# A decoder trunk on one core: a stage for turning the cumulated gates, and a retimed table of small stages

## The chip, the cores and the metric

The kernel runs on one core of one Trainium2 chip. The metric is the device time of one execution in microseconds (us); the median of three runs of the kernel before is 866.67 us (866.63 to 866.77). An execution of this kernel repeats closely, so that a change of 0.2% (1.7 us) can be told from none.

## The reference, cut to what matters

Two layers, 256 tokens, width 1024, all in float32. Each layer is one wide projection, four token mixers, gated sums, an output projection and a SwiGLU block:

```python
proj = einsum('bsd,dn->bsn', rms_norm(x), w_in)        # n = 7428 columns
u, dq, dk, dv, sq, sk, sv, fq, fk, fv, f_logit, g_logit = split(proj)
o_pool = pool_mixer(u); o_diff = diff_attention(dq, dk, dv)
o_sb = stick_breaking(sq, sk, sv)
# forgetting attention: the cumulated log gates are added to the scores
cum = cumsum(log_sigmoid(f_logit + b_forget))
logits = fq_n @ fk_n.T * scale + cum[q] - cum[k]
o_fox = softmax(causal(logits)) @ fv
merged = sum_n sigmoid(g_n + b_gate) * (o_n @ w_branch_n)
x = x + merged @ w_out
h = rms_norm(x); gate, up = split(h @ w_up); x = x + (silu(gate) * up) @ w_down
```

## The kernel before, in words

**Weights and slots.** The weights of one layer are cut into 144 units. A unit is two blocks of 128 rows by 512 columns (260 columns for one item), 512 KB. SyncE loads it into `raw`; ScalarE rounds it into `w_hi` (`split_hi`, L718), VectorE subtracts to get the remainder `w_lo` (`split_lo`, L977), and TensorE multiplies: high by high, high by low, low by high (L1636, L1637, L1640), for both halves of the tokens. That makes 12 matmuls of 512 columns for a unit. The products go into `bulk`, four PSUM banks. The number of a unit in its layer is also the number of its slot. A ring of five buffers (`RING`) holds the split weights: ScalarE splits unit g+4 only when TensorE is done with unit g-1, and VectorE splits unit g+4 at the end of its own slot g.

**Small stages between the units.** Everything that is not a bulk product is a stage: transposes, scores, softmax, evacuations. The tables `MIXING_PE`, `MIXING_ACT` and `MIXING_DVE` say in which slot each engine does its part of which stage. On TensorE the stages of a slot come before the unit of that slot. On ScalarE and VectorE they come before the split of unit g+4. Each engine does its list strictly in order, so an entry that has to wait holds back all behind it, the splits too. The four PSUM banks of the small stages are called A, B, T and O; `take` makes TensorE wait until the last reader of a bank is done with it.

**The stages that the change touches.** `tr_ss` and `ss_evac` turn and evacuate the queries and keys of stick-breaking attention (the four instructions at L1172 and L1174 on VectorE). At slot 8 of layer 0 VectorE also makes the masks (five casts, L1347 and L1349). `tr_fox` turns the forgetting queries (`fq`) or keys (`fk`) into bank A (L1414), and next to them the cumulated gates, `forget_rows`, into bank B (L1415); ScalarE and VectorE evacuate both (`fox_evac`). `scores`, `maxima`, `softmax`, `tr_probs`, `probs_evac`, `pv` and `pv_evac` are the steps of attention, for four `diff` heads and two pairs of `fox` heads. `sigmoid` opens the gates on ScalarE. `tr_diff` and `diff_evac` turn the normalized output of the diff heads. GpSimd turns heads with rotary embedding (L656 to L663) and adds the four gated branches, six additions for each half j of the columns (L690). The additions for the last branch signal `merged_ready`, once for each half t of the tokens. `tr_merged` j waits for `merged_ready` (j, 0), turns that half into one bank, then waits for `merged_ready` (j, 1) and turns the other (L1567). Units 74 to 77 are the first that multiply what `tr_merged` 1 turned.

Of the kernel before, what the change touches and what calls it, by code (L numbers as in the profile page):

```python
# [122 lines left out]
def timetable(*entries):  # L123
# [9 lines left out]
    (32, "scores", "diff", 1), (32, "pv", "diff", 0), (34, "cum"), (34, "pool_a"), (34, "scores", "diff", 2),
    (35, "tr_probs", "diff", 1), (36, "scores", "diff", 3), (36, "pool_b"), (36, "pv", "diff", 1),
    (37, "tr_probs", "diff", 2), (38, "tr_fox", "fq"), (38, "pv", "diff", 2), (39, "tr_fox", "fk"),
    (40, "tr_probs", "diff", 3), (42, "scores", "fox", 0), (42, "pv", "diff", 3), (45, "tr_probs", "fox", 0),
    (45, "scores", "fox", 1), (46, "pv", "fox", 0), (50, "tr_probs", "fox", 1), (52, "tr_diff", 0), (52, "tr_diff", 1),
# [1634 lines left out]
```

## Time and profile before

| | us |
|---|---|
| median of 3 runs | 866.67 |
| the profiled execution, its own time | 866.5 |
| the profiled execution, span from first to last instruction | 864.7 |
| TensorE busy | 860.1 (99%) |
| VectorE busy | 599.4 (69%) |
| ScalarE busy | 441.4 (51%) |
| GpSimd busy | 110.1 (13%) |

The span begins at the first instruction, so all starts below count from there. A busy TensorE row is read with care: matmuls overlap, and the modelled duration of one (0.39 us at 512 columns) is longer than the step from one start to the next (0.23 us). What a matmul costs is that step, not its duration. A short wait can hide in this overlap without showing as idle time.

### The profile page before, as it was taken

Reading aid. Unit: us, or ns where it says so; the run is one execution under the profiler, and the core shown is the slowest. Engines: PE = TensorE matmul, PEld = TensorE weight load, DVE = VectorE, ACT = ScalarE, POOL = GpSimd, SP = SyncE. Lnnn points to the kernel's source line nnn. Section 1 sums busy time; section 2 is a strip of 40 time slices with the busy share of each in tenths; the row PEclk is TensorE's granted clock in tenths of the full one; section 3 lists DMA queues with packets and bytes.
Section 4 is the critical chain, followed back from the end, with each engine's and each line's share of the span. In section 5 each row is a group of like instructions: output and inputs, shape, how many; then the busy total and the mean of one; then the engine's idle time right before and its main releaser. Section 6 shows DMA issues by size and latency. Waiting matters only on the chain.

```text
span 864.7 us, 11127 instructions
## 1 busy us (share of the span) xinstructions
PE 860.1 (99%) x4247; PEld 712.1 (82%) x4247; DVE 599.4 (69%) x847; ACT 441.4 (51%) x639; POOL 110.1 (13%) x89
## 2 busy tenths in 40 slices
PE   9999999999999999999999999999999999999998
PEld 7888888888888888888888888888888888888886
DVE  5996887768777556654479868777597765565542
ACT  6556564754454444443375574556543644444431
POOL 0740100004501000000005401000064000000000
PEclk9999999999999999999999999999999999999999
DMA  9656565575657666555665455655666476665541
GB/s 331 201 185 179 173 189 171 161 236 183 207 171 237 192 178 190 192 175 193 171 184 166 130 183 168 194 176 175 210 195 193 127 238 177 190 185 181 194 146 50
DMA packets 87366, 159.48 MB, mean 184 GB/s; under 512 B 7432, under 2 KB 13712, under 8 KB 87312
## 3 DMA queue, kind: packets, MB, share of 16 engines
q1 hardware_dynamic: 87152, 158.69, 59.1%
q8 instruction: 34, 0.56, 0.2%
q14 instruction: 20, 0.16, 0.1%
q10 hardware_dynamic: 160, 0.07, 0.0%
HBM read 157.69 MB, written 1.05 MB: 184 GB/s over the span
## 4 chain that ended last, share of the span: by engine, by line
PE 99%; DMA 0%; DVE 0%; issue 0%
PE bulk L1636 30%; PE bulk L1640 30%; PE bulk L1637 30%; PE bankAB L1386 2%; PE bulk L1667 1%; PE bankAB L1577 1%; PE bankT L1530 0%; PE bankAB L1519 0%; DMA con<-consts_dram 0%; PE bankAB L1477 0%; PE bankAB L1395 0%; PE bankO L1490 0%; PE bankO L1548 0%; PE bankO L1577 0%; PE bankT L1577 0%; PE bankO L1395 0%
## 5 line engine op out<-in xcount | busy, mean ns | idle before, releaser
L977 DVE TENSOR_TENSOR w_lo<-raw,w_hi 128x1024 fp32r<-128x1024 f32 (+1 forms) x288 | 361.6, 1268 | 162.4 <-ACT w_hi L718 159.8
L718 ACT ACTIVATE w_hi<-raw 128x1024 fp32r<-128x1024 f32 (+1 forms) x288 | 299.0, 1048 | 237.5 <-PE bulk L1640 233.7
L1636 PE MATMUL bulk<-w_hi,hT_hi 128*128 128x512 f32 (+1 forms) x884 | 346.5, 392 | 0.0
L1637 PE MATMUL bulk<-w_lo,hT_hi 128*128 128x512 f32 (+1 forms) x884 | 340.8, 386 | 0.0
L1640 PE MATMUL bulk<-w_hi,hT_lo 128*128 128x512 f32 (+1 forms) x884 | 338.1, 386 | 0.0
L1640 PEld LDWEIGHTS bulk<-w_hi,hT_lo 128*128 128x128 f32 x884 | 165.7, 188 | 33.8
L1636 PEld LDWEIGHTS bulk<-w_hi,hT_hi 128*128 128x128 f32 x884 | 166.1, 188 | 33.3 <-issue 1.6
L1637 PEld LDWEIGHTS bulk<-w_lo,hT_hi 128*128 128x128 f32 x884 | 166.2, 188 | 31.4
L1636 PE MATMUL bulk<-w_hi,aT_hi 128*128 128x512 f32 x176 | 68.8, 391 | 0.0
L1640 PE MATMUL bulk<-w_hi,aT_lo 128*128 128x512 f32 x176 | 68.5, 389 | 0.0
L1637 PE MATMUL bulk<-w_lo,aT_hi 128*128 128x512 f32 x176 | 68.5, 389 | 0.0
L690 POOL TENSOR_TENSOR wide<-wide 128x512 f32<-128x512 f32 x24 | 46.1, 1943 | 125.2 <-DVE wide L1262 124.8
L656 POOL TENSOR_TENSOR wide<-wide,ropeA 128x512 f32<-128x512 f32 x8 | 12.0, 1494 | 210.9 <-DVE wide L1069 210.9
L1640 PEld LDWEIGHTS bulk<-w_hi,aT_lo 128*128 128x128 f32 x176 | 33.0, 188 | 7.0
L1637 PEld LDWEIGHTS bulk<-w_lo,aT_hi 128*128 128x128 f32 x176 | 33.0, 188 | 6.8
L1636 PEld LDWEIGHTS bulk<-w_hi,aT_hi 128*128 128x128 f32 x176 | 33.0, 188 | 6.7
L1636 PE MATMUL bulk<-w_hi,oT_hi 128*128 128x512 f32 x80 | 31.3, 391 | 0.0
L1640 PE MATMUL bulk<-w_hi,oT_lo 128*128 128x512 f32 x80 | 31.1, 389 | 0.0
L1637 PE MATMUL bulk<-w_lo,oT_hi 128*128 128x512 f32 x80 | 31.1, 389 | 0.0
L914 ACT ACTIVATE wide<-bulk,y_ffn 128x512 f32<-128x512 f32 (+1 forms) x24 | 14.4, 651 | 18.2 <-PE bulk L1640 16.0
L1252 DVE SCALAR_TENSOR_TENSOR wide<-bulk,y_attn,bias 128x512 f32<-128x512 f32 x32 | 22.5, 744 | 1.4 <-PE bulk L1640 1.4
L1276 DVE SCALAR_TENSOR_TENSOR wide<-bulk,y_ffn,wide 128x512 f32<-128x512 f32 (+1 forms) x24 | 15.9, 702 | 10.2 <-ACT wide L914 10.2
(259 smaller groups left out, 711.7 us busy)
## 6 DMA issues: line engine op xcount, KB each, us to landing
raw<-in_w_in_dram SPq DMA_DIRECT2D x112, 512.0 KB, 4.4
raw<-in_w_ffn_up_dram SPq DMA_DIRECT2D x80, 512.0 KB, 4.4
raw<-in_w_ffn_down_dram SPq DMA_DIRECT2D x44, 512.0 KB, 3.3
raw<-in_w_branch_dram SPq DMA_DIRECT2D x20, 512.0 KB, 4.1
raw<-in_w_out_dram SPq DMA_DIRECT2D x16, 512.0 KB, 3.3
bias<-in_b_gate_dram SPq DMA_DIRECT2D x16, 256.0 KB, 4.9
raw<-in_w_ffn_up_dram SPq DMA_DIRECT2D x16, 256.0 KB, 3.4
raw<-in_w_in_dram SPq DMA_DIRECT2D x8, 256.0 KB, 2.6
```

The lines of the kernel that those rows point to most:

```text
L656: pool.tensor_tensor(ta, x, ropeA[:, i, t:t + 1, :].broadcast_to([P, 8, HD]), ALU.mult)
L690: ins = pool.tensor_tensor(m, m, wide[:, t, n * D + j * NC:n * D + (j + 1) * NC], ALU.add)
L718: act.activation(w_hi[:, g % RING, :, 0:width], raw[:, g % RAW, :, 0:width], ACT.Copy).then_inc(hi_ready, 1)
L914: act.activation(ff_tmp(t, p, width), item_bank(layer, ITEM_AT[item], t)[:, 0:width], ACT.Sigmoid, scale=y_ffn[:, t:t + 1]).then_inc(ff_si ...
L977: vec.tensor_tensor(w_lo[:, g % RING, :, 0:width], raw[:, g % RAW, :, 0:width], w_hi[:, g % RING, :, 0:width].bitcast(F32), ALU.subtract). ...
L1252: vec.scalar_tensor_tensor(out=wide[:, t, g * NC:(g + 1) * NC], in0=item_bank(layer, ITEM_AT[("gate", g)], t), scalar=y_attn[:, t:t + 1], ...
L1276: vec.scalar_tensor_tensor(out=s, in0=item_bank(layer, ITEM_AT[item], t)[:, 0:width], scalar=y_ffn[:, t:t + 1], in1=s, op0=ALU.mult, op1=A ...
L1386: ins = pe.matmul(dst, a[a_part], b[b_part], start=start and a_part + b_part == 0, stop=stop and a_part == 1, skip_group_check=True)
L1577: ins = pe.transpose(bank[name][:, k * P:(k + 1) * P], ff_act(t, p, blocks * P)[:, k * P:(k + 1) * P], identity)
L1636: pe.matmul(dst, hi, whi, start=(k == ks[0]), stop=False)
L1637: pe.matmul(dst, hi, wlo, start=False, stop=False)
L1640: ins = pe.matmul(dst, lo, whi, start=False, stop=(k == ks[-1]))
```

## The change

1. The gates leave `tr_fox`. It turns queries into bank A and keys into bank B, four transposes each, and no longer waits for the gates. A new stage `tr_forget` turns the gates into bank T, four transposes, with its own evacuation `forget_evac` (two ScalarE copies) and its own signal `forgetsT_ready`, for which the fox scores wait. The numbers of transposes and copies are the same as before.
2. Stages move in the three tables. On TensorE the stages of slots 34 to 54 stood in 13 slots and stand in 9. `tr_qk` dq and `sb_scores` 0 change places in slot 14. `tr_merged` 1 moves from slot 73 to 72. On VectorE `ss_evac` moves from 9 to 7, and in the region from 34 to 56 entries change places. On ScalarE the first `sigmoid` comes ahead of the exponentials of the second pair of fox heads.

The diff, cut to its core; of the tables, the entries named above and a few around them:

```diff
 MIXING_PE = [
-    (9, "tr_ss"), (14, "sb_scores", 0), (14, "tr_qk", "dq"), ...
+    (9, "tr_ss"), (14, "tr_qk", "dq"), (14, "sb_scores", 0), ...
...
-    (54, "pv", "fox", 1), (68, "tr_merged", 0), (73, "tr_merged", 1)]
+    (55, "pv", "fox", 1), (68, "tr_merged", 0), (72, "tr_merged", 1)]
...
 MIXING_ACT = [
-    ... (42, "softmax", "fox", 0), (45, "probs_evac", "fox", 0), (46, "softmax", "fox", 1),
-    (46, "sigmoid", 0, 0), (48, "pv_evac", "fox", 0), (48, "sigmoid", 0, 1), ...
+    ... (42, "softmax", "fox", 0), (44, "probs_evac", "fox", 0),
+    (46, "sigmoid", 0, 0), (47, "softmax", "fox", 1), (48, "pv_evac", "fox", 0), (48, "sigmoid", 0, 1), ...
...
 MIXING_DVE = [
-    (5, "qk_norm", "dq"), (7, "lambda_sums"), (9, "ss_evac"), (10, "lambdas"), ...
+    (5, "qk_norm", "dq"), (7, "lambda_sums"), (7, "ss_evac"), (10, "lambdas"), ...
...
-    (40, "gate", 2), (41, "maxima", "fox", 0),
-    (42, "pv_evac", "diff", 3), (42, "softmax", "fox", 0), (44, "gate", 3), ...
+    (40, "gate", 2), (41, "maxima", "fox", 0),
+    (41, "softmax", "fox", 0), (42, "pv_evac", "diff", 3), (43, "gate", 3), ...
...
+            def forget_evac(layer):
+                act.wait_ge(stage_done, nth(stage_done, layer, ("tr_forget",)))
+                act.activation(forgetsT["fq"], bank["T"][:, 0:SEQ], ACT.Copy)
+                act.activation(forgetsT["fk"], bank["T"][:, SEQ:2 * SEQ], ACT.Copy).then_inc(forgetsT_ready, 1)
...
             def tr_fox(layer, which):
-                pe.wait_ge(forget_out, nth(forget_out, layer, "aug"))
                 pe.wait_ge(rotated, nth(rotated, layer, (which, 1)))
-                take("AB", qkT_ready, layer, which)
+                name = {"fq": "A", "fk": "B"}[which]
+                take(name, qkT_ready, layer, which)
                 for t in range(TT):
                     for pair in range(2):
                         at = pair * SEQ + t * P
-                        pe.transpose(bank["A"][:, at:at + P], foxes[which][:, t, pair * P:(pair + 1) * P], identity)
-                    ins = pe.transpose(bank["B"][:, t * P:(t + 1) * P], forget_window[which, t], identity)
+                        ins = pe.transpose(bank[name][:, at:at + P], foxes[which][:, t, pair * P:(pair + 1) * P], identity)
                 ins.then_inc(stage_done, 1)
...
+            def tr_forget(layer):
+                pe.wait_ge(forget_out, nth(forget_out, layer, "aug"))
+                take("T", forgetsT_ready, layer, "both")
+                for i, which in enumerate(("fq", "fk")):
+                    for t in range(TT):
+                        at = i * SEQ + t * P
+                        ins = pe.transpose(bank["T"][:, at:at + P], forget_window[which, t], identity)
+                ins.then_inc(stage_done, 1)
...
             def scores(layer, kind, h):
...
+                if kind == "fox":
+                    pe.wait_ge(forgetsT_ready, nth(forgetsT_ready, layer, "both"))
```

TensorE around `tr_merged` 1 (transposes out of `wide` into T and O, each waiting for `merged_ready`), before:

```order
L1636 MATMUL bulk<-w_hi,hT_hi 128x512
L1637 MATMUL bulk<-w_lo,hT_hi 128x512
L1640 MATMUL bulk<-w_hi,hT_lo 128x512
L1567 MATMUL bankT<-con,wide 128x128 [waits lhs_lo,merged_ready]
L1567 MATMUL bankT<-con,wide 128x128 x3
L1567 MATMUL bankO<-con,wide 128x128 [waits lhs_lo,merged_ready]
L1567 MATMUL bankO<-con,wide 128x128 x3
L1636 MATMUL bulk<-w_hi,hT_hi 128x512 [waits lo_ready]
```

The same place now:

```order
L1653 MATMUL bulk<-w_hi,hT_hi 128x512
L1654 MATMUL bulk<-w_lo,hT_hi 128x512
L1657 MATMUL bulk<-w_hi,hT_lo 128x512
L1584 MATMUL bankT<-con,wide 128x128 [waits lhs_lo,merged_ready]
L1584 MATMUL bankT<-con,wide 128x128 x3
L1584 MATMUL bankO<-con,wide 128x128 [waits lhs_lo,merged_ready]
L1584 MATMUL bankO<-con,wide 128x128 x3
L1653 MATMUL bulk<-w_hi,hT_hi 128x512 [waits gated,lo_ready]
```

The eight transposes now stand ahead of unit 72, whose first matmul is the one that waits for `gated`; before, unit 72 stood ahead of them. Between the two `tr_merged` stages there were five units, now there are four.

VectorE from slot 7 to slot 10 of layer 0, before (L977 are the splits of units 11, 12 and 13, `keys_lo` is `ss_evac`, `small` belongs to `lambda_sums`, the casts make the masks):

```order
L1098 TENSOR_REDUCE small<-wide 128x2 [waits vec_step]
L977 TENSOR_TENSOR w_lo<-raw,w_hi 128x1024 [waits hi_ready]
L1347 CAST masks<-con 128x128 [waits consts_loaded]
L1347 CAST masks<-con 128x128 x2
L1349 CAST sums<-con 128x128 x2
L977 TENSOR_TENSOR w_lo<-raw,w_hi 128x1024 [waits hi_ready]
L1172 SCALAR_TENSOR_TENSOR keys_lo<-bankT,keys_hi 128x2x128 [waits sT_hi]
L1174 TENSOR_TENSOR keys_lo<-bankT,keys_hi 128x2x128
L1172 SCALAR_TENSOR_TENSOR keys_lo<-bankO,keys_hi 128x2x128 [waits sT_hi]
L1174 TENSOR_TENSOR keys_lo<-bankO,keys_hi 128x2x128
L977 TENSOR_TENSOR w_lo<-raw,w_hi 128x1024 [waits hi_ready]
```

The same place now:

```order
L1104 TENSOR_REDUCE small<-wide 128x2 [waits vec_step]
L1178 SCALAR_TENSOR_TENSOR keys_lo<-bankT,keys_hi 128x2x128 [waits sT_hi]
L1180 TENSOR_TENSOR keys_lo<-bankT,keys_hi 128x2x128
L1178 SCALAR_TENSOR_TENSOR keys_lo<-bankO,keys_hi 128x2x128 [waits sT_hi]
L1180 TENSOR_TENSOR keys_lo<-bankO,keys_hi 128x2x128
L983 TENSOR_TENSOR w_lo<-raw,w_hi 128x1024 [waits hi_ready]
L1353 CAST masks<-con 128x128 [waits consts_loaded]
L1353 CAST masks<-con 128x128 x2
L1355 CAST sums<-con 128x128 x2
L983 TENSOR_TENSOR w_lo<-raw,w_hi 128x1024 [waits hi_ready] x2
```

The four instructions of `ss_evac` now stand ahead of the splits of units 11 and 12.

ScalarE around the second pair of fox heads (`sb,den<-bankAB` are its exponentials, `wide<-wide` the sigmoids), before:

```order
L870 ACTIVATE sb,den<-bankAB,nmx 128x256 [waits probs_ready,maxed]
L872 ACTIVATE sb,den<-bankAB,nmx 128x128
L870 ACTIVATE sb,den<-bankAB,nmx 128x256
L872 ACTIVATE sb,den<-bankAB,nmx 128x128
L896 ACT_TABLE_LOAD
L896 ACTIVATE wide<-wide 128x1024 [waits gate_ready]
```

Now:

```order
L902 ACT_TABLE_LOAD
L902 ACTIVATE wide<-wide 128x1024 [waits gate_ready]
L719 ACTIVATE w_hi<-raw 128x1024 [waits unit_done,raw_loaded2]
L876 ACT_TABLE_LOAD [waits probs_ready]
L876 ACTIVATE sb,den<-bankAB,nmx 128x256 [waits maxed]
L878 ACTIVATE sb,den<-bankAB,nmx 128x128
L876 ACTIVATE sb,den<-bankAB,nmx 128x256
L878 ACTIVATE sb,den<-bankAB,nmx 128x128
L719 ACTIVATE w_hi<-raw 128x1024 [waits unit_done,raw_loaded3]
L723 ACTIVATE oT_hi<-bankO 128x256 [waits stage_done]
L902 ACT_TABLE_LOAD
```

A sigmoid now stands between two sets of exponentials, and two more table loads stand in each layer.

## Rows read from the trace of the kernel before

**Rows 1.** Page, parts 1 and 2: busy times; granted clock in tenths, 40 slices.

```profile
PE 860.1 (99%) x4247; PEld 712.1 (82%) x4247; DVE 599.4 (69%) x847; ACT 441.4 (51%) x639; POOL 110.1 (13%) x89
...
PEclk9999999999999999999999999999999999999999
```

**Rows 2.** Waits of TensorE: line, waited for, us in total, times, longest.

```profile
PE bulk L1674 <- DVE warm L1311: 1.0, 1, 1.0
```

**Rows 3.** Timeline of TensorE, slots 72, 73, and 73 of layer 1: start us, us, engine, line, operation.

```profile
230.27 0.39 PE L1636 MATMUL bulk<-w_hi,hT_hi 128*128 128x512 f32 x1
...
233.00 0.60 PE L1567 MATMUL bankT<-con,wide 128*128 128x128 f32 x4
233.43 0.60 PE L1567 MATMUL bankO<-con,wide 128*128 128x128 f32 x4
233.79 0.47 PE L1636 MATMUL bulk<-w_hi,hT_hi 128*128 128x512 f32 x1
...
660.00 0.60 PE L1567 MATMUL bankT<-con,wide 128*128 128x128 f32 x4
```

**Rows 4.** Timeline of GpSimd, the last addition of half 1, layers 0 and 1.

```profile
229.59 2.27 POOL L690 TENSOR_TENSOR wide<-wide 128x512 f32<-128x512 f32 x1
...
656.59 2.28 POOL L690 TENSOR_TENSOR wide<-wide 128x512 f32<-128x512 f32 x1
```

**Rows 5.** Timeline of VectorE, the split beside the addition of layer 0.

```profile
228.90 1.81 DVE L977 TENSOR_TENSOR w_lo<-raw,w_hi 128x1024 fp32r<-128x1024 f32 x1 [0.42 <-ACT w_hi L718]
```

**Rows 6.** Timeline of VectorE, slots 7 to 9 of layer 0.

```profile
36.97 2.00 DVE L977 TENSOR_TENSOR w_lo<-raw,w_hi 128x1024 fp32r<-128x1024 f32 x1
...
40.27 0.21 DVE L1347 CAST masks<-con 128x128 bf16<-128x128 f32 x1
40.41 1.31 DVE L1349 CAST sums<-con 128x128 fp32r<-128x128 f32 x1
...
41.77 1.21 DVE L977 TENSOR_TENSOR w_lo<-raw,w_hi 128x1024 fp32r<-128x1024 f32 x1
42.91 0.41 DVE L1172 SCALAR_TENSOR_TENSOR keys_lo<-bankT,keys_hi 128x256 fp32r<-128x256 f32 x1
...
44.24 1.21 DVE L977 TENSOR_TENSOR w_lo<-raw,w_hi 128x1024 fp32r<-128x1024 f32 x1
```

**Rows 7.** Timeline of GpSimd beside them (rotary embedding).

```profile
36.55 1.35 POOL L656 TENSOR_TENSOR wide<-wide,ropeA 128x512 f32<-128x512 f32 x1
...
40.34 1.29 POOL L663 TENSOR_TENSOR wide<-wide 128x512 f32<-128x512 f32 x1
```

**Rows 8.** Timeline of TensorE's weight loads and matmuls, start of unit 12.

```profile
43.04 0.19 PEld L1636 LDWEIGHTS bulk<-w_hi,hT_hi 128*128 128x128 f32 x1
...
43.16 0.40 PE L1636 MATMUL bulk<-w_hi,hT_hi 128*128 128x512 f32 x1
```

**Rows 9.** Timeline of TensorE, the first two matmuls after the transposes of slot 39.

```profile
130.97 0.47 PE L1636 MATMUL bulk<-w_hi,hT_hi 128*128 128x512 f32 x1
131.28 0.39 PE L1637 MATMUL bulk<-w_lo,hT_hi 128*128 128x512 f32 x1
```

**Rows 10.** Timeline of VectorE, the divisions (`softmax`) of fox pairs 0 and 1.

```profile
144.34 0.18 DVE L1197 RECIPROCAL inverse<-den 128x4 f32<-128x4 f32 x1 [0.32 <-ACT sb L872]
...
146.65 2.35 DVE L977 TENSOR_TENSOR w_lo<-raw,w_hi 128x1024 fp32r<-128x1024 f32 x2
...
159.87 0.17 DVE L1197 RECIPROCAL inverse<-den 128x4 f32<-128x4 f32 x1
...
161.00 0.42 DVE L984 TENSOR_TENSOR oT_lo<-bankO,oT_hi 128x256 fp32r<-128x256 f32 x1
```

**Rows 11.** Timeline of TensorE, `tr_probs` of fox pair 0 in slot 45.

```profile
150.00 0.49 PE L1530 MATMUL bankT<-con,sb 128*128 128x128 f32 x3
```

**Rows 12.** Timeline of ScalarE, end of the exponentials and the table load.

```profile
155.16 0.22 ACT L872 ACTIVATION_READ_ACCUMULATOR sb<-bankAB,nmx 128x1 f32 x1
155.39 1.28 ACT L896 ACT_TABLE_LOAD   x1
```

More of the change, by code:

```diff
@@ L130 @@
 MIXING_PE = [
-    (9, "tr_ss"), (14, "sb_scores", 0), (14, "tr_qk", "dq"), (18, "sb_sums", 0), (20, "sb_out", 0), (20, "sb_scores", 1),
+    (9, "tr_ss"), (14, "tr_qk", "dq"), (14, "sb_scores", 0), (18, "sb_sums", 0), (20, "sb_out", 0), (20, "sb_scores", 1),
     (23, "sb_sums", 1), (24, "tr_qk", "dk"), (25, "sb_out", 1), (25, "scores", "diff", 0), (29, "tr_probs", "diff", 0),
[L133 to L137, printed above, removed]
-    (54, "pv", "fox", 1), (68, "tr_merged", 0), (73, "tr_merged", 1)]
+    (32, "scores", "diff", 1), (32, "pv", "diff", 0), (35, "cum"), (35, "pool_a"), (35, "scores", "diff", 2),
+    (35, "tr_probs", "diff", 1), (37, "scores", "diff", 3), (37, "pool_b"), (37, "pv", "diff", 1),
+    (39, "tr_probs", "diff", 2), (39, "tr_fox", "fq"), (39, "tr_fox", "fk"), (39, "pv", "diff", 2), (39, "tr_forget"),
+    (42, "tr_probs", "diff", 3), (42, "scores", "fox", 0), (42, "pv", "diff", 3), (44, "tr_probs", "fox", 0),
+    (46, "pv", "fox", 0), (46, "scores", "fox", 1), (51, "tr_probs", "fox", 1), (53, "tr_diff", 0), (53, "tr_diff", 1),
+    (55, "pv", "fox", 1), (68, "tr_merged", 0), (72, "tr_merged", 1)]
 _PE = [(0, "tr_norm", "attn", 0, 1)] + MIXING_PE + [(F0, "tr_norm", "ffn", 0, 1)]
@@ L210 @@
-    (50, "probs_evac", "fox", 1), (52, "diff_evac", 0), (52, "diff_evac", 1), (52, "sigmoid", 2, 0),
-    (54, "pv_evac", "fox", 1), (54, "sigmoid", 2, 1), (60, "sigmoid", 3, 0), (61, "sigmoid", 3, 1), (69, "merged_evac", 0),
+    (36, "pool_evac_a"), (36, "probs_evac", "diff", 1), (36, "softmax", "diff", 2), (37, "pool_evac_b"),
+    (38, "softmax", "diff", 3), (38, "probs_evac", "diff", 2), (39, "fox_evac", "fq"), (39, "fox_evac", "fk"),
+    (39, "forget_evac"), (41, "probs_evac", "diff", 3), (42, "softmax", "fox", 0), (44, "probs_evac", "fox", 0),
@@ L486, in build @@
         qkT_ready = signal("qkT_ready", turned)
+        forgetsT_ready = signal("forgetsT_ready", ["both"])
         qkT_hi = signal("qkT_hi", turned)
@@ L1162, in fox_evac @@
                 high, low = (part[:, 0:2, :] for part in qT[which])
-                vec.tensor_tensor(low, bank["A"].rearrange("p (h q) -> p h q", h=2), high.bitcast(F32),
-                                  ALU.subtract).then_inc(qkT_ready, 1)
+                src = bank[{"fq": "A", "fk": "B"}[which]].rearrange("p (h q) -> p h q", h=2)
+                vec.tensor_tensor(low, src, high.bitcast(F32), ALU.subtract).then_inc(qkT_ready, 1)
             def ss_evac(layer):
@@ L1305, in _ @@
                           sb_mask=sb_mask, fox_norm=fox_norm,
-                          sb_weights=nothing, sb_evac=sb_evac, fox_evac=fox_evac, fkfv=nothing, dv=nothing,
+                          sb_weights=nothing, sb_evac=sb_evac, forget_evac=nothing, fox_evac=fox_evac, fkfv=nothing, dv=nothing,
                           softmax=softmax, probs_evac=nothing, pv_evac=pv_evac, diff_norm=diff_norm,
@@ L1578, in tr_act @@
                     ins.then_inc(stage_done, 1)
-            stages = dict(tr_norm=tr_norm, tr_qk=tr_qk, tr_fox=tr_fox, tr_ss=tr_ss, cum=cum, pool_a=pool_a, pool_b=pool_b,
+            stages = dict(tr_norm=tr_norm, tr_qk=tr_qk, tr_fox=tr_fox, tr_forget=tr_forget, tr_ss=tr_ss, cum=cum, pool_a=pool_a, pool_b=pool_b,
                           sb_scores=sb_scores, sb_sums=sb_sums, sb_out=sb_out, scores=scores, tr_probs=tr_probs, pv=pv,
```

38 lines of the change are left out of this document (18 added, 20 removed).

## Prediction

> **What bounds the kernel.** I read the busy times first. TensorE is at work for 860.1 of 864.7 us, VectorE for 69%, ScalarE for 51%, and the granted clock is at its full 2.4 GHz level in all forty slices [rows 1]. Then the waits: all that TensorE ever waited for in a way that shows is 1.0 us at the start, ahead of the warm-up [rows 2]. So nothing can be won by making another engine faster, and an edit acts in two ways only: it changes what TensorE has to do, or it makes TensorE wait where it did not. The profiled execution took 866.5 us; I sum against that and carry the sum to the median, 866.67.
>
> Then the timelines, for how close each hand-over is. The price of a bulk matmul is the step between starts. From 230.27 to 233.00 lie the twelve of unit 72: 2.73 us, 0.23 each [rows 3]. A slot without stages is 2.73 us long, and this is the unit in which I move things.
>
> **The edit itself: gates in bank T.** Per layer, twelve transposes stay twelve and four ScalarE copies stay four; matmuls and bytes are the same. What changes is what waits for what. The new wait of the fox scores for `forgetsT_ready` ends two slots before the scores: `tr_forget` stands in slot 39, the scores in slot 42, and between them lie three units, 8.2 us, for two copies. Behind `forget_evac` on ScalarE stands the split of unit 43, with four units' time to spare. I cost this edit at nothing. Its cover is those three units; without it the copies, under 1 us, would be paid.
>
> **Fewer visits.** TensorE leaves the bulk products for the stages of slots 34 to 54 thirteen times a layer, then nine times. Going back costs something: the first matmul after transposes takes 0.31 us to the next start (130.97 to 131.28) where 0.23 is usual [rows 9], so 0.08 us. Bounds for a visit saved: below, nothing (the last transpose before the unit may be started past more quickly and give it back); above, 0.2, if going in costs as much as coming out and a little more. I take 0.08, the row's own number: 4 visits x 2 layers x 0.08 = 0.64 us won, between 0 and 1.6. The swap in slot 14 leaves the number of visits alone: nothing.
>
> **`tr_merged` 1, one slot earlier.** It turns the two halves of the merged gates, four transposes each. Before, the first group starts at 233.00 and the second at 233.43 [rows 3], and the second needs GpSimd's last addition, which ends at 229.59 + 2.27 = 231.86 [rows 4]: 1.57 us to spare. In layer 1 it ends at 658.87, and the first group starts at 660.00 [rows 3, 4]: in either layer the addition ends 1.13 to 1.14 us ahead of the first group. Unit 72 was the cover. Now the first group starts at 230.27, in place of that unit. Its addition is done by 229.59, when the last one starts. The second group comes 0.43 later, at 230.70, and waits until 231.86. A weight load then follows 0.06 us behind a release and the first matmul 0.12 behind the load: unit 12 shows it, 42.98 to 43.04 to 43.16 [rows 6, 8]. So it starts at 232.04 and not at 230.70: 1.34 us lost, which no later place gives back, since TensorE has no idle time into which it could be pushed.
>
> Is the addition tied to TensorE, so that it doesn't come earlier too? GpSimd's additions wait for VectorE's products with the gates, and these wait for units 65 to 69; the tables leave that order alone. The split beside the last addition itself waits for ScalarE (0.42 us), which waits for TensorE [rows 5]. So the whole chain moves with TensorE. Per layer 1.34 us, with bounds 1.1 (the release is seen at once, and the weight load is hidden) and 1.4; two layers: 2.7 us.
>
> **`ss_evac` ahead of two splits.** VectorE's four instructions take 44.24 - 42.91 = 1.33 us [rows 6]. They now run at 36.97, before the splits of units 11 and 12. Their input is there (ScalarE has evacuated the same banks by then). In layer 0 the split of unit 12 ends at 41.77 + 1.21 = 42.98, the weight load starts at 43.04 and the matmul at 43.16, just 0.23 after its predecessor's start: not late, but with nothing to spare [rows 6, 8]. Above, the whole 1.33 is paid. Below, nothing: much of VectorE's time here is waiting. The split at 36.97 takes 2.00 us where 1.21 is usual, and ends 1.07 after GpSimd's instruction that began at 36.55 ended at 37.90. One cast takes 0.21, the next 1.31, up to 41.72, just behind the end of GpSimd's instruction at 40.34 + 1.29 = 41.63 [rows 6, 7]. So an instruction of VectorE that reads SBUF waits for the one of GpSimd that is running. `ss_evac` reads PSUM beside SBUF and took its plain time. While it runs, GpSimd gets ahead: behind 37.90 it has two instructions of half width and the one of 1.29, some 2.8 us, and the split of unit 11 holds it up for 1.1, so it is done at about 41.8 (an estimate from these rows). By then two of the five casts are through, three follow at 0.21, and the split of unit 12 begins at about 42.2 and ends at about 43.4. Loss: 0.4 us, the value I take, between 0 and 1.33. In layer 1 there are no casts in this place, and unit 12's split has several us to spare: nothing.
>
> [...]
>
> **Slots 34 to 56.** I followed each hand-over with the steps above. The closest new one is in slot 44. `tr_probs` of fox pair 0 moves from 150.00 [rows 11] to about 147.2, and needs bank O, so VectorE's copy of the last diff head's output. In the VectorE list that copy now stands behind the division of pair 0 and the split of unit 45, which were behind it. The exponentials end at 144.3; the division takes 1.13 if it runs as for pair 1 (159.87 to 161.00), 2.31 if as for pair 0 (144.34 to 146.65) [rows 10]; split and copy take 1.2 + 0.4. That gives 147.0 or 148.2. The division of pair 0 was slow because GpSimd's squares ran beside it, and these wait for that same copy, so they can't now. I take 147.0: nothing lost. The other end is 1.0 us a layer. The next closest is `pv` of diff head 2 in slot 39, in the same slot as its `tr_probs`; eight transposes of `tr_fox` (0.9 us) lie between and cover the evacuation.
>
> **Sum.** -0.64 + 2.68 + 0.4 = +2.4 us: 868.9 for a profiled execution, 869.1 as a median.
>
> **Rivals.**
> (a) *The addition is done in time: not slower.* Should GpSimd's last additions take 1.3 us like its instruction at 40.34 [rows 7], and not 2.27, the last two end 1.9 us sooner, at about 229.9, before 230.70. Then nothing is paid in slot 72, and -0.64 + 0.4 remains: 866.4, no change. It decides if the additions are done by 230.6. For it: VectorE's entries before shift, and its split beside the addition (1.81 us and not 1.21 [rows 5]) shows that the two hold each other up. Against it: the lists of both engines after slot 60 are untouched, and the two layers agree to 0.01 us. 10%.
> (b) *The copy in slot 44 is late too.* As above with the slow division, 0.5 to 1.0 a layer: 870 to 871.1. 10%.
> (c) *The table loads.* ScalarE now changes tables three times, not once, around the second fox pair. A load takes 1.28 us and begins as the exponentials end (155.38 to 155.39) [rows 12]. Two more are 2.6 us of ScalarE, which was idle longer than that between slots 42 and 50, and the fox probabilities of pair 1 then come about 1.7 us before slot 51 needs them: nothing. If loads cost twice that, TensorE waits 1 to 2 us a layer in slot 51: 871 to 873. 4%.
> The Trainium skill, "ScalarE: Activation LUTs", section "What ACT_TABLE_LOAD costs", puts a switch at 2.66 us, 1.28 for the load and as much again for a drain. The row shows the load and no drain before it, so I keep (c) small.
> (d) *Fewer visits count for more,* with (a)'s additions in time: faster by over 0.2%. 3%.
>
> **Chances and range.** The forecast's mechanism, `merged_ready` late in slot 72 in both layers, has 73%. Its own range goes from 2.2 - 1.6 + 0 = +0.6 to 2.8 + 1.33 = +4.1, and I believe its middle: 868 to 870.5. With (b) above and part of (a) below: 867.3 to 871. A difference of 0.2% (1.7 us, so above 868.4 or below 864.9) is what can be told from none. Slower: nearly all of the forecast (68 of 73), (b) and (c), 80%. No change: (a) and the forecast's low end, 17%. Faster: 3%.
>
> **What would show it.** In the profile after, the waits of TensorE list L1584 waiting for GpSimd's L690, once a layer. A modelled matmul end hides some of it, so the starts tell more: from the first group of `tr_merged` 1 to the second, about 1.8 us and not 0.43. In layer 0 the step into unit 12 is 0.6 us and not 0.23, in layer 1 it is 0.23. There is no step over 0.4 us at slots 39, 44 and 51. From slot 34 to slot 56 TensorE takes some 0.3 us less in each layer. The prediction is wrong if the second group follows the first without a gap, or if a gap stands anywhere else.

## The result, and the profile after

The changed kernel takes 868.52 us (median of 14 runs, 868.38 to 868.96), the kernel before 866.56 (14 runs, 866.25 to 866.78): 1.96 us or 0.23% more, a ratio of 1.0023 with a 95% interval of 1.0016 to 1.0030. It is slower, as forecast, by 1.96 us where 2.4 were forecast. The profiled execution took 868.38 us, with a span of 866.6, against 866.5 and 864.7.

The page of the changed kernel, beside [rows 1], shows TensorE at work for 99% of the span again; ScalarE has four instructions more, the table loads.

```profile
PE 859.9 (99%) x4247; PEld 712.7 (82%) x4247; DVE 594.5 (69%) x847; ACT 447.3 (52%) x643; POOL 111.7 (13%) x89
```

The list of TensorE's waits of the changed kernel (us in total, times, longest) has a new first line beside [rows 2]: the second group of `tr_merged` 1 waits for GpSimd's addition, once in each layer. The other two lines are of the start of the program. The kernel before has both as well, the second with 0.4 us (`consts_dram`), which the prediction left out when it put all of TensorE's visible waiting at 1.0.

```profile
PE bankO L1584 <- POOL wide L691: 2.1, 2, 1.0
PE bulk L1691 <- DVE warm L1317: 1.0, 1, 1.0
PE bankO L1697 <- DMA con<-consts_dram: 0.5, 1, 0.5
```

The timelines of GpSimd, TensorE and its weight loads in slot 72 of the changed kernel, and one row of layer 1, answer to [rows 3, 4]:

```profile
229.26 2.25 POOL L691 TENSOR_TENSOR wide<-wide 128x512 f32<-128x512 f32 x1
...
229.94 0.60 PE L1584 MATMUL bankT<-con,wide 128*128 128x128 f32 x4
231.57 0.66 PE L1584 MATMUL bankO<-con,wide 128*128 128x128 f32 x4 [1.03 <-POOL wide L691]
231.98 0.47 PE L1653 MATMUL bulk<-w_hi,hT_hi 128*128 128x512 f32 x1
...
231.57 0.42 PEld L1584 LDWEIGHTS bankO<-con,wide 128*128 128x128 f32 x4 [1.26 <-POOL wide L691]
...
659.56 0.66 PE L1584 MATMUL bankO<-con,wide 128*128 128x128 f32 x4 [1.02 <-POOL wide L691]
```

The addition ends at 229.26 + 2.25 = 231.51, and 0.06 later the second group starts, 1.63 us behind the first and not 0.43. The wait shows as 1.03 only, because the modelled end of the first group covers the rest: the steps are what to read. From unit 9 to unit 143 of either layer this is also the only place of the changed kernel where two starts of TensorE in a row lie over 0.35 us apart; in the kernel before there is none.

Where does the time go? Most of it can be told by the first matmul of a unit: a stretch between two such starts repeats within 0.04 us in kernels that don't differ there; the one exception behind the start-up is the 2.7 us from unit 12 to 13 of layer 0, which varies by 0.06. From the timelines of TensorE of both kernels, in us:

| units | before | after | difference | what differs there |
|---|---|---|---|---|
| start to 9, layer 0 | 34.90 | 34.65 | -0.25 | start-up, 34.65 to 35.17 over all kernels here |
| 9 to 16, layer 0 | 21.04 | 21.27 | +0.23 | `ss_evac`, slot 14 |
| 16 to 32 | 47.81 | 47.86 | +0.05 | entries of slots 16 to 21 |
| 32 to 56 | 82.11 | 81.74 | -0.37 | the visits, the gates |
| 56 to 68 | 33.43 | 33.43 | 0 | |
| 68 to 74 | 17.35 | 18.60 | +1.25 | `tr_merged` 1 |
| 0 to 143, layer 1 | | | +0.98 | the same, without `ss_evac` |

In layer 0 that is +1.16 from unit 9 on, in layer 1 +0.98; with the start-up's -0.25 it makes 1.89 of 1.88 us (868.38 - 866.5). The start-up differs by up to 0.5 us between the profiled executions, also among kernels that are the same up to there, so differences of 0.1 or 0.2 us are read from the stretches and not from the whole time.

### The profile page after: what moved, and what is told of

Same layout as the page of the kernel before. It is cut to its first block, busy times and chain, and to the rows that moved or that the text cites. A ratio compares the mean times of both kernels' runs of the same rounds, so it can differ in the third digit from the quotient of the medians.

```text
span 866.6 us, 11133 instructions
## 1 busy us (share of the span) xinstructions
PE 859.9 (99%) x4247; PEld 712.7 (82%) x4247; DVE 594.5 (69%) x847; ACT 447.3 (52%) x643; POOL 111.7 (13%) x89
## 4 chain that ended last, share of the span: by engine, by line
PE 96%; DVE 1%; POOL 1%; issue 1%; DMA 0%; POOLq 0%
PE bulk L1653 29%; PE bulk L1657 29%; PE bulk L1654 29%; PE bankAB L1392 2%; PE bulk L1684 1%; POOL wide L691 1%; DVE wide L1268 1%; PE bankAB L1594 1%; PE bankT L1547 0%; PE bankAB L1536 0%; DMA con<-consts_dram 0%; DVE w_lo L983 0%; PE bankAB L1492 0%; PE bankAB L1401 0%; DVE hT_lo L990 0%
## 5 line engine op out<-in xcount | busy, mean ns | idle before, releaser
L691 POOL TENSOR_TENSOR wide<-wide 128x512 f32<-128x512 f32 x24 | 46.1, 1941 | 117.0 <-DVE wide L1268 116.5
```

The source lines that it names most:

```text
L691: ins = pool.tensor_tensor(m, m, wide[:, t, n * D + j * NC:n * D + (j + 1) * NC], ALU.add)
```

## Experiments

Each group of kernels was timed together with the kernel before on one chip. The times are medians; "against before" is the difference of medians within the same group. The ratio goes by means, and so can differ a little from the medians: kernel 9 had two executions of 867.18 and 867.68 us among eleven.

| kernel | us | runs | against before | ratio, 95% interval |
|---|---|---|---|---|
| 1 changed, `tr_merged` 1 in 73 | 866.19 | 11 | -0.40 | 0.9996, 0.9987 to 1.0005 |
| 2 before, `tr_merged` 1 in 72 | 869.08 | 7 | +2.49 | 1.0028, 1.0017 to 1.0039 |
| 3 as 1, `ss_evac` in 9 | 866.02 | 11 | -0.57 | 0.9991, 0.9982 to 1.0000 |
| 4 before, `ss_evac` in 7 | 866.70 | 11 | +0.11 | 1.0001, 0.9992 to 1.0010 |
| 5 before, the gates' edit alone | 866.50 | 11 | -0.11 | 0.9999, 0.9990 to 1.0008 |
| 6 before, `tr_merged` 1 in 71 | 879.56 | 2 | +12.95 | 1.0149, 1.0131 to 1.0168 |
| 7 as 3, first sigmoid later | 867.61 | 11 | +1.00 | 1.0012, 1.0003 to 1.0020 |
| 8 as 3, `tr_merged` 1 in halves, 72 and 73 | 866.06 | 11 | -0.55 | 0.9994, 0.9985 to 1.0002 |
| 9 as 3, all sigmoids behind `pv_evac` | 866.03 | 11 | -0.49 | 0.9998, 0.9989 to 1.0007 |
| 10 as 8, halves in 71 and 73 | 872.80 | 2 | +6.28 | 1.0072, 1.0054 to 1.0091 |
| 11 changed, short last addition | 866.45 | 10 | -0.07 | 0.9999, 0.9990 to 1.0008 |
| 12 as 3, slots 14 to 21 as before | 865.74 | 11 | -0.83 | 0.9990, 0.9981 to 0.9999 |

### 1 and 2: `tr_merged` 1 put back, and moved alone

```diff
-    (55, "pv", "fox", 1), (68, "tr_merged", 0), (72, "tr_merged", 1)]
+    (55, "pv", "fox", 1), (68, "tr_merged", 0), (73, "tr_merged", 1)]
```

> The changed kernel with tr_merged 1 back in slot 73. Theory 1 (the loss is TensorE's wait in slot 72 for GpSimd's last addition): the step from the first to the second group of tr_merged 1 falls from 1.63 to 0.43 us in both layers, 2.4 us less than the changed kernel, so about 866.1 us, 0.4 to 0.5 below the kernel before. Theory 2 (the loss comes from what moved in slots 34 to 56, the table loads among it, and from slots 7 to 14, and the slot of tr_merged only decides where it shows): about 868.5, as the changed kernel.

In the kernel before, the opposite edit:

```diff
-    (54, "pv", "fox", 1), (68, "tr_merged", 0), (73, "tr_merged", 1)]
+    (54, "pv", "fox", 1), (68, "tr_merged", 0), (72, "tr_merged", 1)]
```

> The kernel before with tr_merged 1 in slot 72 and nothing else. Theory 1: plus 1.2 us a layer, 2.4 in all, about 869.0 us, more than the whole change cost; the second group starts 1.6 us behind the first. Theory 2: no difference from the kernel before.

Put back, the kernel loses the whole excess: 866.19, 2.3 us below the changed kernel. The two groups of transposes follow each other without a wait; TensorE's timeline of kernel 1:

```profile
233.00 0.60 PE L1584 MATMUL bankT<-con,wide 128*128 128x128 f32 x4
233.43 0.60 PE L1584 MATMUL bankO<-con,wide 128*128 128x128 f32 x4
```

Moved alone, in the kernel before, the stage costs 2.49 us, more than the whole change. TensorE's timeline of kernel 2 shows the wait as in the changed kernel:

```profile
230.28 0.60 PE L1567 MATMUL bankT<-con,wide 128*128 128x128 f32 x4
231.90 0.66 PE L1567 MATMUL bankO<-con,wide 128*128 128x128 f32 x4 [1.02 <-POOL wide L690]
```

From unit 68 to unit 74 both kernels with slot 72 take 18.58 to 18.60 us in either layer, both with slot 73 take 17.34 to 17.35. Theory 2 has fallen.

### 11: the last two additions made short

The kernel adds only half of the columns of the last branch in half 1 and leaves the other half out, so its output is not that of the reference; it serves to move the end of the additions alone.

```diff
-                            m = merged(t)[:, j * NC:(j + 1) * NC]
-                            ins = pool.tensor_tensor(m, m, wide[:, t, n * D + j * NC:n * D + (j + 1) * NC], ALU.add)
+                            w = NC // 2 if (j, n) == (1, 3) else NC
+                            m = merged(t)[:, j * NC:j * NC + w]
+                            ins = pool.tensor_tensor(m, m, wide[:, t, n * D + j * NC:n * D + j * NC + w], ALU.add)
```

> The changed kernel, tr_merged 1 in slot 72, with GpSimd's two additions of the last branch in half 1 cut to half their columns (the other half of that branch is left out of the sum, so the output isn't the reference's). They then take about 1.1 us and not 2.25 each and end at 229.3 of layer 0, before the second group's turn at 230.35. Theory 1 (the last addition is what slot 72 waits for): the second group follows 0.43 behind the first, and the time is that of the changed kernel with tr_merged 1 in 73, 866.2. Rival: the wait ends with something else that only comes at the same time (ScalarE's evacuation, VectorE's product): the step stays 1.6 us, 868.5.

866.45 us with `tr_merged` 1 still in slot 72: the slot itself costs nothing, the addition does. GpSimd's and TensorE's timelines of this kernel:

```profile
227.42 3.37 POOL L692 TENSOR_TENSOR wide<-wide 128x256 f32<-128x256 f32 x2
...
230.29 0.60 PE L1585 MATMUL bankT<-con,wide 128*128 128x128 f32 x4
230.84 0.66 PE L1585 MATMUL bankO<-con,wide 128*128 128x128 f32 x4
```

Half the columns take not half the time: the two end at 230.79, not at 229.3 as I expected, and the second group follows at 230.84, 0.12 late. So even here the start of the group follows the end of the addition by 0.05 us. From unit 68 to 74 this kernel takes 17.51 us in layer 0 and 17.48 in layer 1, where kernel 1 takes 17.34 in both: 0.31 us in all, about the difference between the two against before (-0.07 and -0.40).

### 8: only the second group has to wait

The first half of the stage in slot 72, the second in 73:

```diff
-    (55, "pv", "fox", 1), (68, "tr_merged", 0), (73, "tr_merged", 1)]
+    (55, "pv", "fox", 1), (68, "tr_merged", 0), (72, "tr_merged", 1, 0), (73, "tr_merged", 1, 1)]
...
-            def tr_merged(layer, j):
-                for t in range(TT):
+            def tr_merged(layer, j, *halves):
+                for t in halves or range(TT):
```

> The changed kernel with ss_evac in 9 and tr_merged 1 in two halves: its first group of transposes in slot 72, its second in 73. My reading: only the second group waits for the last addition; in slot 73 it has 1.1 us to spare, so only one more visit a layer is paid, 0.1 us each: 866.2. Rival: being in slot 72 is what costs (the first group waits too, or the unit behind it does): up to 2.4 us more, 868.4.

866.06 us, as kernel 3 with both halves in 73. The first group starts at 230.00, the second at 233.20, and TensorE's list of waits has neither. One more visit a layer was expected to cost 0.2 us in all and doesn't show (0.05 us between units 68 and 74 of layer 0). The rival has fallen.

### 3, 4 and 12: `ss_evac`, and what I had put at nothing

The expectations call "port reading" what the prediction read from the rows: an instruction of VectorE that reads SBUF waits for the one of GpSimd that is running, and `ss_evac` fills a time that VectorE would have waited. The "plain shift" would have all behind `ss_evac` later by its 1.33 us.

```diff
-    (5, "qk_norm", "dq"), (7, "lambda_sums"), (7, "ss_evac"), (10, "lambdas"), ...
+    (5, "qk_norm", "dq"), (7, "lambda_sums"), (9, "ss_evac"), (10, "lambdas"), ...
```

> The changed kernel with tr_merged 1 in slot 73 and VectorE's ss_evac back in slot 9. What is left of the change is then the visits and the gates. Port reading (ss_evac ahead of the splits of units 11 and 12 costs layer 0 a little): 0.1 to 0.4 us less than with tr_merged 1 alone put back, 865.8 to 866.0. Plain shift of VectorE's list: 1.3 less. If ss_evac costs nothing: the same as that kernel. In the trace the steps into units 11 to 14 of layer 0 are 0.23 us again.

Kernel 4 is the kernel before with the opposite edit:

```diff
-    (5, "qk_norm", "dq"), (7, "lambda_sums"), (9, "ss_evac"), (10, "lambdas"), ...
+    (5, "qk_norm", "dq"), (7, "lambda_sums"), (7, "ss_evac"), (10, "lambdas"), ...
```

> The kernel before with ss_evac in VectorE's slot 7 and nothing else. Port reading with the traces of both kernels: plus 0.1 to 0.2 us, in layer 0 alone (my prediction had 0.4): 866.7. Plain shift: plus 1.3, 867.9.

Kernel 3 is 0.17 us below kernel 1, kernel 4 is 0.11 above before. A plain shift of the list by 1.33 us has fallen. The timelines of VectorE, GpSimd and TensorE (weight load, then matmuls) of the changed kernel there, beside [rows 6 to 8]:

```profile
38.03 1.38 DVE L983 TENSOR_TENSOR w_lo<-raw,w_hi 128x1024 fp32r<-128x1024 f32 x1
39.34 2.13 DVE L1353 CAST masks<-con 128x128 bf16<-128x128 f32 x3
41.39 0.35 DVE L1355 CAST sums<-con 128x128 fp32r<-128x128 f32 x2
41.66 2.34 DVE L983 TENSOR_TENSOR w_lo<-raw,w_hi 128x1024 fp32r<-128x1024 f32 x2
...
37.59 0.74 POOL L658 TENSOR_TENSOR wide<-wide,ropeB 128x256 f32<-128x256 f32 x1
38.29 1.72 POOL L660 TENSOR_TENSOR wide<-wide,ropeB 128x256 f32<-128x256 f32 x1
40.09 1.29 POOL L664 TENSOR_TENSOR wide<-wide 128x512 f32<-128x512 f32 x1
...
42.92 0.19 PEld L1653 LDWEIGHTS bulk<-w_hi,hT_hi 128*128 128x128 f32 x1 [0.28 <-DVE w_lo L983]
...
42.68 0.39 PE L1657 MATMUL bulk<-w_hi,hT_lo 128*128 128x512 f32 x1
42.92 0.50 PE L1653 MATMUL bulk<-w_hi,hT_hi 128*128 128x512 f32 x1
43.26 0.40 PE L1654 MATMUL bulk<-w_lo,hT_hi 128*128 128x512 f32 x1
```

The first three casts end at 41.47, just behind GpSimd's last instruction (40.09 + 1.29 = 41.38), as the port reading says. The casts read one SBUF operand, the splits two, and both kinds are held up (a cast takes 0.21 us, or 1.31 when it is held up [rows 6]); `ss_evac`, which reads PSUM beside SBUF, isn't. From 36.71, where `ss_evac` begins, to the end of the split of unit 12 at 42.87 lie 6.16 us; in the kernel before the same work without `ss_evac` took 6.01 (36.97 to 42.98 [rows 6]). So 1.18 of its 1.33 us went into time that VectorE had waited.

I had the split of unit 12 begin at 42.2; it begins at 41.66. Some 0.26 us of that is the earlier start-up, which TensorE shares and which gains nothing. GpSimd needs 3.75 us from its hand-over at 36.29 + 1.34 = 37.63 to 41.38 and not 3.9, and then 0.28 us of casts are left and not 0.4, since three of the five are through and not two. So the split is 0.14 us late and not 0.4. The step into unit 12 is 0.24 us and not the 0.6 that I named as a sign: the weight load waits for the split, and 0.1 more shows one step later (42.92 to 43.26).

From unit 12 to 13 the kernels with `ss_evac` in 7 take 2.90 (changed, kernel 1), 2.86 (kernel 11) and 2.76 us (kernel 4), before and kernels 3, 5, 8 and 12, with 9, take 2.72 to 2.78. Against before's 2.74 that is a cost of 0.02 to 0.16 us. VectorE and GpSimd run in the same pattern in all four (the split 1.38 or 1.39, three casts 2.13 or 2.14). What differs is how far ahead TensorE is: unit 9 begins 1.86 us before VectorE's `small` reduction in the changed kernel and kernels 1 and 11 (34.65 and 36.51), 1.71 before it in kernel 4 (35.12 and 36.83). Kernel 4's step is inside the spread of the kernels without the move, and in its profiled execution all that it is above before lies in the start-up.

What remained in kernel 3 against before from unit 13 to unit 25 was 0.11 us a layer. Kernel 12 takes the other entries of slots 14 to 21 back too:

```diff
-    (9, "tr_ss"), (14, "tr_qk", "dq"), (14, "sb_scores", 0), ...
+    (9, "tr_ss"), (14, "sb_scores", 0), (14, "tr_qk", "dq"), ...
...
-    ... (16, "sb_weights", 0), ... (21, "sb_split", 1), (21, "sb_evac", 0), ...
+    ... (17, "sb_weights", 0), ... (21, "sb_evac", 0), (21, "sb_split", 1), ...
...
-    ... (20, "sb_split", 1), ...
+    ... (19, "sb_split", 1), ...
```

> The changed kernel with tr_merged 1 in 73 and ss_evac in 9, and also sb_scores 0 ahead of tr_qk dq in slot 14 and the entries of slots 16 to 21 as in the kernel before; what is left of the change is the gates' edit and slots 32 to 56. In all traces with the changed order unit 14 begins 0.03 to 0.04 us later behind unit 13, unit 15 0.03 later behind unit 14, and slots 20 to 25 take 0.04 more, in each layer. My prediction had put slot 14 at nothing. If that is the order, slots 13 to 25 take the times of before again, 0.2 us less in all: 865.8, the lowest of the kernels here. If it is chance from run to run: 866.0 and the same steps.

865.74 us, the lowest of all, 0.83 below before with an interval that excludes no difference (0.9981 to 0.9999). The steps are those of before again: unit 13 to 14 4.49 (4.53 in kernel 3), 14 to 15 2.84 (2.86), 20 to 25 16.52 (16.56). TensorE's timeline in slot 14 of the changed kernel shows a part of it:

```profile
48.54 0.60 PE L1410 MATMUL bankT<-con,wide 128*128 128x128 f32 x4
...
50.34 0.50 PE L1653 MATMUL bulk<-w_hi,hT_hi 128*128 128x512 f32 x1
50.68 0.39 PE L1654 MATMUL bulk<-w_lo,hT_hi 128*128 128x512 f32 x1
```

Behind scores, whose weights have 64 rows, the first step of the unit takes 0.34 us; behind transposes it takes 0.31 [rows 9]. The order of stages inside a visit has a price, if a small one.

### 5: the gates' edit alone

```diff
-    (37, "tr_probs", "diff", 2), (38, "tr_fox", "fq"), (38, "pv", "diff", 2), (39, "tr_fox", "fk"),
+    (37, "tr_probs", "diff", 2), (38, "tr_fox", "fq"), (38, "pv", "diff", 2), (39, "tr_fox", "fk"), (39, "tr_forget"),
```

with the bodies of the changed kernel, `forget_evac` behind `fox_evac`, and the tables of before otherwise.

> The kernel before with the gates' edit alone: tr_forget in slot 39 behind tr_fox fk, forget_evac behind fox_evac, and all other entries in the slots of before, so that TensorE still visits its stages thirteen times between slots 34 and 56. My reading: the gates' edit is worth nothing and the visits make the 0.36 us a layer, so the time is that of the kernel before, 866.6, and from slot 34 to slot 56 of layer 0 TensorE takes 76.5 us. Rival: the gates' edit makes the gain (transposes of one stage write one bank, not two in turn), then 76.2 us, and 865.9.

866.50 us, and 82.10 us from unit 32 to 56, where before has 82.11 and every kernel with nine visits but kernel 7 81.70 to 81.74. The gates' edit is worth nothing; what else moved in slots 32 to 56 is worth 0.37 us in layer 0 and 0.35 in layer 1. That this is the number of visits was not tested alone, since entries of ScalarE and VectorE moved too; but TensorE waits nowhere in this stretch in either kernel, and its steps fit: the first matmul behind a visit takes 0.32 us in the mean to the next, 13 times before and 9 times after, where others take 0.23. The first matmuls of units 32 and 56 in the timelines of the kernel before, kernel 5 and the changed kernel:

```profile
103.75 0.48 PE L1636 MATMUL bulk<-w_hi,hT_hi 128*128 128x512 f32 x1
...
185.86 0.39 PE L1636 MATMUL bulk<-w_hi,hT_hi 128*128 128x512 f32 x1
```

```profile
103.91 0.48 PE L1653 MATMUL bulk<-w_hi,hT_hi 128*128 128x512 f32 x1
...
186.01 0.39 PE L1653 MATMUL bulk<-w_hi,hT_hi 128*128 128x512 f32 x1
```

```profile
103.78 0.48 PE L1653 MATMUL bulk<-w_hi,hT_hi 128*128 128x512 f32 x1
...
185.52 0.39 PE L1653 MATMUL bulk<-w_hi,hT_hi 128*128 128x512 f32 x1
```

### 7 and 9: the table loads

```diff
-    (46, "sigmoid", 0, 0), (47, "softmax", "fox", 1), (48, "pv_evac", "fox", 0), (48, "sigmoid", 0, 1), ...
+    (47, "softmax", "fox", 1), (47, "sigmoid", 0, 0), (48, "pv_evac", "fox", 0), (48, "sigmoid", 0, 1), ...
```

> The changed kernel with tr_merged 1 in 73 and ss_evac in 9, and the first sigmoid behind the exponentials of the second fox pair, so that ScalarE loads its tables two times fewer in each layer. My reading: a load of 1.28 us lies in ScalarE's spare time, so no difference from the same kernel without this edit, 866.0. Rival (c): each load holds TensorE's next stage back by something; then up to 2 us less.

My expectation fell: with two loads fewer in a layer, the kernel is 1.6 us slower than kernel 3. The timelines of ScalarE, VectorE and TensorE of kernel 7 show why:

```profile
160.18 1.06 ACT L902 ACTIVATE wide<-wide 128x1024 f32<-128x1024 f32 x1
...
162.09 0.36 ACT L723 ACTIVATE oT_hi<-bankO 128x256 fp32r<-128x256 f32 x1
...
162.48 0.42 DVE L990 TENSOR_TENSOR oT_lo<-bankO,oT_hi 128x256 fp32r<-128x256 f32 x1 [4.25 <-ACT oT_hi L723]
...
170.03 0.55 PE L1547 MATMUL bankT<-con,sb 128*128 128x128 f32 x3 [0.55 <-DVE sb L1219]
```

ScalarE's evacuation of pair 0 now stands behind a sigmoid and begins at 162.09, in kernel 3 at 159.86. VectorE's half of it begins at 162.48 and not 160.28, and in VectorE's list `diff_norm` and the division of pair 1 stand behind. So the division is 2.2 us later, with 1.7 to spare: TensorE waits in slot 51, which costs 0.8 us in each layer from unit 50 to 56. Kernel 9 puts the sigmoid behind that evacuation instead:

```diff
-    (47, "softmax", "fox", 1), (47, "sigmoid", 0, 0), (48, "pv_evac", "fox", 0), (48, "sigmoid", 0, 1), ...
+    (47, "softmax", "fox", 1), (48, "pv_evac", "fox", 0), (48, "sigmoid", 0, 0), (48, "sigmoid", 0, 1), ...
```

> The changed kernel with tr_merged 1 in 73 and ss_evac in 9, and all sigmoids behind ScalarE's evacuation of pair 0 (pv_evac fox 0), so that two table loads a layer go and nothing stands ahead of that evacuation. The kernel with the first sigmoid merely behind the exponentials lost 1.6 us; two readings. If the cause was the order (ScalarE's evacuation of pair 0 behind the sigmoid, and VectorE's division of pair 1 behind that evacuation), the evacuation is early again, the division is 1.7 us ahead of slot 51, and the time is 866.0. If the place of the table loads itself matters (one load less ahead of the exponentials, all four sigmoids in a row hold back ScalarE's splits), it stays at about 867.6.

```profile
160.00 0.39 ACT L723 ACTIVATE oT_hi<-bankO 128x256 fp32r<-128x256 f32 x1
160.40 1.28 ACT L902 ACT_TABLE_LOAD   x1
161.70 2.01 ACT L902 ACTIVATE wide<-wide 128x1024 f32<-128x1024 f32 x2
```

866.03 us, as kernel 3, with 639 ScalarE instructions and not 643. The order was the cause, and table loads cost nothing here in either direction.

### 6 and 10: a longer wait, and the clock

```diff
-    (54, "pv", "fox", 1), (68, "tr_merged", 0), (73, "tr_merged", 1)]
+    (54, "pv", "fox", 1), (68, "tr_merged", 0), (71, "tr_merged", 1)]
```

> The kernel before with tr_merged 1 two slots earlier, in 71. If the wait ends with GpSimd's last addition, whose time is tied to the units before slot 70 and not to slot 72, a second slot costs its whole length: the second group starts 1.6 + 2.7 = 4.4 us behind where it could, 3.9 us a layer more than before (1.2 + 2.73), 7.9 in all, about 874.5 us. Rival: the additions come earlier when tr_merged does, or a wait ahead of ScalarE's splits stretches it; then the cost per layer isn't 1.2 + 2.73.

It cost 12.95 us, not 7.9. The waits are as expected; what comes behind them isn't. TensorE's timeline of kernel 6:

```profile
229.47 0.66 PE L1567 MATMUL bankT<-con,wide 128*128 128x128 f32 x4 [1.95 <-POOL wide L690]
231.68 1.12 PE L1567 MATMUL bankO<-con,wide 128*128 128x128 f32 x4 [1.55 <-POOL wide L690]
232.44 0.78 PE L1636 MATMUL bulk<-w_hi,hT_hi 128*128 128x512 f32 x1
233.01 0.63 PE L1637 MATMUL bulk<-w_lo,hT_hi 128*128 128x512 f32 x1
233.44 0.63 PE L1640 MATMUL bulk<-w_hi,hT_lo 128*128 128x512 f32 x1
...
237.70 0.40 PE L1636 MATMUL bulk<-w_hi,hT_hi 128*128 128x512 f32 x1
237.93 0.40 PE L1637 MATMUL bulk<-w_lo,hT_hi 128*128 128x512 f32 x1
```

The group at 229.47 still takes 0.66 us, the one at 231.68 takes 1.12, and the twelve matmuls from 232.44 to 237.70 have steps of 0.43 us and not 0.23, about 2.5 us more in each layer: the granted clock fell to its 1.2 GHz level. Kernel 10 keeps one of the two waits:

```diff
-    ... (68, "tr_merged", 0), (72, "tr_merged", 1, 0), (73, "tr_merged", 1, 1)]
+    ... (68, "tr_merged", 0), (71, "tr_merged", 1, 0), (73, "tr_merged", 1, 1)]
```

> The changed kernel with ss_evac in 9, the first half of tr_merged 1 in slot 71 and the second in 73. The first group waits 1.95 us for its addition, as in the kernel with both in 71, the second doesn't wait. Reading 1: the clock fell there because of the two waits together (3.5 us in 4.5), so here it holds and the cost is 2.1 us a layer for the wait and 0.1 for the visit: 866.0 + 4.4 = 870.4. Reading 2: one wait of 2 us is enough for the lower clock, which adds 2.4 us a layer (twelve steps of 0.43 for 0.23): 875.

The two executions took 872.02 and 873.58 us, between the readings. In the profiled one the same wait stands in both layers, and the stretch behind it (us, busy times, granted clock, DMA share, GB/s) runs at the full level in layer 0 and at the low one in layer 1:

```profile
229.51 0.65 PE L1584 MATMUL bankT<-con,wide 128*128 128x128 f32 x4 [1.95 <-POOL wide L691]
...
658.44 0.65 PE L1584 MATMUL bankT<-con,wide 128*128 128x128 f32 x4 [1.95 <-POOL wide L691]
```

```profile
229.90:232.70 2.80, 2.80 (x15) 2.35 (x14) 1.33 (x2) 0.60 (x1) 1.79 (x1) 1.00 0.90 296
658.80:662.50 3.70, 3.70 (x13) 2.89 (x12) 1.36 (x2) 0.60 (x1) 1.81 (x1) 0.56 0.99 363
```

From unit 68 to 74 layer 0 takes 19.52 us (2.17 more than before: the wait of 2.1 and a visit), layer 1 21.12: another 1.6. So neither reading holds as I put it: a wait of 1.95 us can bring the lower clock and doesn't always. The other execution, without a trace, took 1.56 us more, and its mean granted clock was 0.996 and not 0.998: what a second layer at the low level would give. If so, the clock fell in three of four places. What decides is open.

## Why the prediction was right, and where its sizes were off

The side and the mechanism were right; the sum was 0.4 to 0.5 us too high. Some 0.3 of that are sizes (two losses were taken too large, a smaller one was left out), the rest lies in the start-up. Step by step:

- *What bounds the kernel.* Right. Every 0.1 us of TensorE's steps came back in the total, and every other engine's extra work (table loads, later copies) cost nothing as long as TensorE didn't wait.
- *The edit itself: nothing.* Right by kernel 5. `forgetsT_ready` appears in no wait.
- *Fewer visits: -0.64, measured -0.72* (0.37 and 0.35), or 0.09 us a visit and not 0.08, if it is the visits. Kernel 8's added visit cost 0.05 or less, so a visit isn't one fixed price.
- *`tr_merged` 1: +2.68, measured +2.50* (2 x 1.25, in the changed kernel and in kernel 2 alike). The size was off by the 0.12 us that I put between weight load and matmul: the four transposes' load and matmul rows both start 0.06 us behind the release. In unit 12 of the kernel before the matmul stood 0.12 behind its load only because its turn came then, 0.23 behind its predecessor; it was not waiting for the load. The addition moved with TensorE, as argued: it ends 0.35 us earlier than before in layer 0, and the first group's turn comes 0.33 earlier than unit 72's did [rows 3, 4].
- *`ss_evac`: +0.4, measured +0.02 to +0.16.* The term that was off the most. The port reading gave the right kind of answer; of the excess, 0.15 us was GpSimd's end taken too late and 0.12 one cast too many behind it. How much is paid hangs on 0.15 us between VectorE and TensorE, which comes out of the start-up and differs between the traces.
- *Slot 14: nothing.* Wrong, by 0.07 us a layer, and 0.04 more for the entries of slots 16 to 21, which the prediction didn't speak of: 0.2 us in all, by kernel 12.
- *Slots 34 to 56: no new wait.* Right: no step there is over 0.35 us, the signs at slots 39, 44 and 51 included. The closest hand-over, VectorE's copy for slot 44, came out at the end that I took. The timelines of VectorE and TensorE of the changed kernel:

```profile
146.53 0.41 DVE L1226 COPY o_d<-bankO 128x256 f32<-128x256 f32 x1
...
147.17 0.49 PE L1547 MATMUL bankT<-con,sb 128*128 128x128 f32 x3
147.50 0.49 PE L1547 MATMUL bankO<-con,sb 128*128 128x128 f32 x3
```

  The copy ends at 146.94, the group into bank O starts at 147.50.

With the measured sizes the sum is 2.50 + 0.16 - 0.72 + 0.22 = 2.16 us, and the stretches behind the start-up show 1.16 + 0.98 = 2.14. What this is above the 1.88 of the profiled execution is the start-up, where the changed kernel happened to be 0.25 us faster. That my 2.44 came within 0.3 us of the 2.14 is in part luck: the 0.22 of slots 14 to 21, which I had at nothing, make up for half of the 0.42 that I had too much for `tr_merged` 1 and `ss_evac`. The chances were added up loosely: 68 of the forecast, 10 of (b) and 4 of (c) make 82% for slower, not 80.

Of the rivals, (a) would have needed additions of 1.3 us; the last one took 2.25. Kernel 11 shows that its mechanism is real: a shorter addition makes slot 72 free. (b) didn't happen. (c) has fallen by kernel 9: four loads fewer leave the time as it is. The Trainium skill, "ScalarE: Activation LUTs", section "What ACT_TABLE_LOAD costs", puts a drain of 1.38 us beside each load. The trace doesn't agree: in kernel 9 the load begins 0.01 us behind the end of the evacuation (160.00 + 0.39, 160.40), and the sigmoids begin 0.02 us behind the 1.28 us load (160.40 + 1.28, 161.70). For (d), the visits count for a little more than I took, far too little to turn the sign.

## What to carry to other kernels

Where one engine is busy throughout, price a moved stage by two things first: the time from its new turn to the end of the last thing that it needs, and the number of times the engine changes kind of work. One slot of 2.73 us turned 1.57 us to spare into 1.2 us of waiting, in two layers, and ate over three times what the four saved visits gave. An edit that bundles many moves should be taken apart before it is judged: of this one, the moves in slots 32 to 56 are worth 0.7 to 0.8 us, once three others are left out. And where two engines hold each other up, a stage that isn't held up itself can go into the waiting for little: `ss_evac` cost at most 0.16 of its 1.33 us.

## What the runs showed of the hardware

A wait can have a second price behind it. Waits that show as 1.03 us and cost 1.2 by the starts (changed kernel, kernel 2) left the granted clock at its full level (1.00 from 231 to 234 and from 659 to 662); one that shows as 1.95, or 2.1 by the starts, brought the 1.2 GHz level in one of two layers, for some 3.3 us at 0.2 us more a matmul; waits of 1.95 and 1.55 us in a row brought it in both layers, for 5.2 us. So a wait that is a little longer can cost nearly twice its length: 3.8 us in layer 1 of kernel 10 for a wait of 2.1. These are four places with traces in two kernels, and no rule is drawn from them.

GpSimd's additions of 128 x 512 (L691) took 1.29 us at the least and 2.25 in the median, in one kernel. The same line at half the width took 1.7 us (3.37 for two) in kernel 11, where an instruction of that width takes 0.74 in other places (37.59). So the part that comes of running beside VectorE is the same 0.96 us at either width, and cutting work there brought much less than half.
